# Two transformer-like blocks on one core: the value product in column halves, z gated from its bank, memories prepared at half rate, the second mixer's weight splits on VectorE

## What is computed

```python
# first block
x = x + hybrid_mixer(rms_norm(x), ...)
x = x + memory_cross_attention(rms_norm(x), rms_norm(mem), ...)
x = x + swiglu_ffn(rms_norm(x), ...)            # then rms_norm(x, norm_final_g)
# second block
x = x + 0.5 * swiglu(...)
x = x + concat([y_hgrn, y_conv]) @ w_out        # y_conv = zb * causal_conv3(zc * zu)
x = x + cross attention to a second memory
x = x + 0.5 * swiglu(...)                        # then rms_norm_2(x, final_norm)

# hybrid_mixer
z, xbc, dt_f, dt_b, q, k, v, gates = split_cols(h @ w_in, IN_SPLITS)
y = y_fwd + y_bwd + d_skip * xh                  # two state-space scans, forward and backward
v_ = (y * silu(z)) by 4 groups of 512 columns; v_ * rsqrt(mean(v_ * v_) + EPS) * g
out = softmax(q k^T, window of 128 and a sink) @ v        # 4 kv heads of 64, 4 q heads each
```

## Time and profile before

| | us |
|---|---|
| median of 3 runs | 2532.95 (2527.86 to 2536.98) |
| the profiled execution | 2534.28 |
| its span | 2532.5 |
| PE busy | 2462.1 (97%) |
| DVE, ACT, POOL busy | 1247.7 (49%), 1005.0 (40%), 394.6 (16%) |
| mean granted clock of PE | 0.989 |

### The profile page before, as it was taken

One profiled execution on the slowest core, in us unless ns is written; L12 is line 12 of the kernel. 1 busy time (PEld: TensorE's weight loads), 2 busy tenths in 40 slices (PEclk: granted clock), 3 DMA queues, 4 the chain that ended last, 5 costly groups with the idle time before them and its releaser, 6 DMA issues.

```text
span 2532.5 us, 29084 instructions
## 1 busy us (share of the span) xinstructions
PE 2462.1 (97%) x11416; PEld 1986.0 (78%) x11416; DVE 1247.7 (49%) x1843; ACT 1005.0 (40%) x1632; POOL 394.6 (16%) x283
## 2 busy tenths in 40 slices
PE   8999999898999999999999999999999999999998
PEld 7766668676888887888888788888887787888886
DVE  5577744457776454533333433423576644444422
ACT  6666653335455233423223322322634333332321
POOL 0000000054410010111102211101455300111101
PEclk9999999999999999999999999999999999999999
DMA  5221225223446331333332233322321222333231
GB/s 183 86 59 49 77 93 188 85 95 106 150 134 216 108 133 50 97 94 93 100 107 93 78 98 100 100 92 92 99 67 51 89 103 67 100 100 98 93 101 50
DMA packets 171337, 251.56 MB, mean 99 GB/s; under 512 B 11201, under 2 KB 88257, under 8 KB 171201
## 3 DMA queue, kind: packets, MB, share of 16 engines
q1 hardware_dynamic: 170768, 248.92, 31.0%
q10 hardware_dynamic: 432, 0.79, 0.1%
HBM read 231.83 MB, written 16.78 MB: 98 GB/s over the span
## 4 chain that ended last, share of the span: by engine, by line
PE 81%; DVE 8%; issue 5%; ACT 4%; DMA 1%; POOL 1%; POOLq 0%; SPq 0%; ACTq 0%; DVEq 0%
PE bank L1058 80%; DVE W L1817 1%; DVE T L1825 1%; DVE wlo L1817 1%; DMA scr_z<-T 1%; ACT whi L1384 1%; PE bank L1161 0%; ACT pr L1479 0%; DVE SC L2428 0%; DVE pr L1928 0%; POOL acc L2511 0%; ACT qs L1384 0%; DMA zb<-scr_z 0%; DVE T L1817 0%; ACT xp L1684 0%
## 5 line engine op out<-in xcount | busy, mean ns | idle before, releaser
L1058 PE MATMUL bank<-xh,whi 128*128 128x512 f32 x1784 | 716.2, 401 | 11.1 <-DVE wlo L1817 10.6
L1058 PE MATMUL bank<-xh,wlo 128*128 128x512 f32 x1784 | 698.5, 392 | 0.0
L1058 PE MATMUL bank<-xl,whi 128*128 128x512 f32 x1784 | 698.0, 391 | 0.0
L1817 DVE TENSOR_TENSOR wlo<-raw,whi 128x1024 fp32r<-128x1024 f32 (+2 forms) x382 | 472.4, 1241 | 332.3 <-ACT whi L1384 332.1
L1384 ACT ACTIVATE whi<-raw 128x1024 fp32r<-128x1024 f32 (+2 forms) x406 | 419.9, 1039 | 539.4 <-PE bank L1058 530.4
L1058 PEld LDWEIGHTS bank<-xh,whi 128*128 128x128 f32 x1784 | 337.1, 189 | 105.5 <-issue 27.2
L1058 PEld LDWEIGHTS bank<-xh,wlo 128*128 128x128 f32 x1784 | 336.7, 189 | 72.2
L1058 PEld LDWEIGHTS bank<-xl,whi 128*128 128x128 f32 x1784 | 337.5, 189 | 66.1 <-issue 1.0
L1817 DVE TENSOR_TENSOR T<-bank,R 128x512 f32<-128x512 f32 x90 | 61.8, 688 | 341.7 <-PE bank L1058 341.7
L1058 PE MATMUL bank<-hh,whi 128*128 128x512 f32 x528 | 205.4, 389 | 0.0
L1058 PE MATMUL bank<-hl,whi 128*128 128x512 f32 x528 | 205.4, 389 | 0.0
(11 more groups left out here) (340 smaller groups left out, 3614.2 us busy)
## 6 DMA issues: line engine op xcount, KB each, us to landing
raw<-in_w_in SPq DMA_DIRECT2D x92, 512.0 KB, 3.6
raw<-in_w_ffn_in SPq DMA_DIRECT2D x88, 256.0 KB, 3.2
raw<-in_ffn_gate SPq DMA_DIRECT2D x88, 256.0 KB, 2.8
raw<-in_ffn_up SPq DMA_DIRECT2D x88, 256.0 KB, 3.1
raw<-in_ffn_down SPq DMA_DIRECT2D x44, 512.0 KB, 3.5
raw<-in_w_ffn_out SPq DMA_DIRECT2D x22, 512.0 KB, 3.5
raw<-in_w_xattn_kv SPq DMA_DIRECT2D x16, 512.0 KB, 4.1
raw<-in_w_kv_mem SPq DMA_DIRECT2D x16, 512.0 KB, 4.0
```

The source lines that it names most:

```text
L1058: return e.matmul(out, l, r, start=start, stop=stop, skip_group_check=skip)
L1817: return e.tensor_tensor(out, a, b, op)
```

## The change

It has seven parts. (A) `pv` writes heads 0 and 2 to partitions 0 to 63 and heads 1 and 3 to 64 to 127, as two products of 256 columns each, and `o_out` is one copy. (B) `z_out` is a tanh straight from the bank with half of Rn as its scale (`Rh`, computed once on DVE), `z_silu` multiplies (tanh + 1) with the bank itself and frees it, and `z_gate` brings in the factor Rh in place of 0.5; one T is used for each tile. (C) Memory 1 is prepared at rate 4 with 8 and 3 empty points, in place of rate 8 with 16 and 7. (D) Memory 2 goes at rate 3 in place of 4; the memories' root is taken 5 points later, its spread one point after it and not two, and a group's `y_mean` and `y_scale` are not taken when its squares are ready, but just ahead of the next memory's root (the last group's when it is ready). (E) What is pending of these is written out between the scan's end and the mark "ssd", with `settle()`. (F) The second mixer's 24 wlo are on DVE; `c_out` multiplies by R², `u_out` multiplies the bank of hu with cu; the first tap is on ACT (`u_first`), the other two on DVE go straight to cu, and POOL's copy is gone; `h_states` stands at the first level of the next head, after its `select`. (G) The last norm's square 6 is added on DVE, not on POOL.

```diff
@@ z's ring, means @@
             soon(1, square)
             if c == 3:
-                soon(2, "y_mean", g)
-                soon(4, "y_scale", g)
+                soon(2, means.append, g)
+            if c == g == 3:
+                soon(2, mean)
+
+        def mean():
+            for g in means:
+                step("y_mean", g)
+                soon(2, "y_scale", g)
+            means.clear()
...
-            for _ in range(7):
+            for _ in range(3):
                 yield
             for k in range(8):
                 step("m_split", tag, k)
...
         def memory(tag):
-            late.append(norm(f"m{tag}", lag=2, among=ELSE))
+            first = norm(f"m{tag}", among=ELSE)
+            def root():
+                mean()
+                first()
+            late.append(lambda: soon(5, root))
...
-                start(prepare(2, 0), 4)
+                start(prepare(2, 0), 3)
...
-                start(prepare(1, 16), 8)
+                start(prepare(1, 8), 4)
...
             step("x_again")
+        mean()
+        settle()
         step("mark", "ssd")
...
             def conv():
-                tmp.new("uc", m)
-                step("u_conv", m)
+                step("u_first", m)
+                soon(1, "u_conv", m)
...
-                if li == 6 and h < 4:
+                h -= 1
+                if h >= 0 and h < 4 and li == 0:
                     side.new("hst", h)
                     step("h_states", h)
-                h -= 1
...
@@ pv, o_out @@
-                    ins = mm(b[0:64, :], v[:, k0 + j, kv * 64:kv * 64 + 64], pt[j][:], j == 0, j == k1 - k0 - 1)
+                    x = pt[j][:].rearrange("p (a b q) -> p a b q", a=2, b=2)
+                    for half in range(2):
+                        ins = mm(b[64 * half:64 * half + 64, 0:256], v[:, k0 + j, kv * 64:kv * 64 + 64], x[:, :, half, :],
+                                 j == 0, j == k1 - k0 - 1)
...
-                copy(q[0:64, 2 * kv:2 * kv + 2, chunk(n)], src[:, :, 0, :]).then_inc(*up("o_out", ("o half", i)))
-                copy(q[64:128, 2 * kv:2 * kv + 2, chunk(n)], src[:, :, 1, :]).then_inc(
+                copy(q[:, 2 * kv:2 * kv + 2, chunk(n)], b[:, 0:256].rearrange("p (a q) -> p a q", a=2)).then_inc(
...
@@ z_out, z_silu, z_gate @@
-                copy(t[:], b[:], Rn[:, m:m + 1]).then_inc(*up("z_act", ("z out", g, m), ("main", "free", u)))
-                w.wait_ge(*free(tmp, "tmp", n2))
-                w.wait_ge(*at("z out", g, m))
-                e.activation(t2[:], t[:], ACT.Tanh, scale=0.5).then_inc(*up("z_act", ("z tanh", g, m)))
+                e.activation(t[:], b[:], ACT.Tanh, scale=Rh[:, m:m + 1]).then_inc(*up("z_act", ("z tanh", g, m)))
...
-                stt(t[:], t2[:], 1.0, t[:], ALU.add, ALU.mult).then_inc(
-                    *up("z_silu", ("z silu", g, m), ("tmp", "free", n2)))
+                stt(t[:], t[:], 1.0, b[:], ALU.add, ALU.mult).then_inc(
+                    *up("z_silu", ("z silu", g, m), ("main", "free", u)))
...
-                stt(x, x, 0.5, z[:], ALU.mult, ALU.mult).then_inc(*up("y_scaled", ("z gated", g, c)))
+                stt(x, x, Rh[:, c:c + 1], z[:], ALU.mult, ALU.mult).then_inc(*up("y_scaled", ("z gated", g, c)))
...
@@ second mixer @@
-            weights(n, columns("w_in_2", i), 8, "mix2", "dve" if n == "hf" else "pool", nat=n == "hi")
+            weights(n, columns("w_in_2", i), 8, "mix2", nat=n == "hi")
...
-                tt(cu[:, m, :], b[:], R[:], ALU.mult).then_inc(*up("mixer2_in", ("c out", m), ("main", "free", u)))
+                tt(cu[:, m, :], b[:], R2[:], ALU.mult).then_inc(*up("mixer2_in", ("c out", m), ("main", "free", u)))
...
-                tt(t[:], b[:], R[:], ALU.mult).then_inc(*up("mixer2_in", ("u out", m), ("main", "free", u)))
-                w.wait_ge(*at("u out", m))
-                w.wait_ge(*at("c out", m))
-                tt(cu[:, m, :], cu[:, m, :], t[:], ALU.mult).then_inc(*up("mixer2_in", ("u in", m), ("tmp", "free", n)))
+                tt(t[:], b[:], cu[:, m, :], ALU.mult).then_inc(*up("mixer2_in", ("u out", m), ("main", "free", u)))
...
+            def u_first(m):
+                n, t = tmp("u", m)
+                w.wait_ge(*at("u out", m))
+                copy(cu[:, m, :], t[:], V("cw2", 3 * m + 2)).then_inc(*up("u_first", ("u conv", m, 0)))
...
@@ square on DVE @@
-                if k == 0 or tag in ("m1", "m2") or (k < 7 and tag != "mix") or tag == "fin":
+                if k == 0 or tag in ("m1", "m2") or (k != (6 if tag == "fin" else 7) and tag != "mix"):
                     return
```

More of the change, by code:

```diff
@@ L129, in build @@
         small = at_kb(116.5, [P, 64], name="small")
-        Rn, Rmn = small[:, 0:4], small[:, 4:6]
+        Rn, Rmn, Rh = small[:, 0:4], small[:, 4:6], small[:, 40:44]
         Rn1, Rn2, Rn3 = small[:, 8:12], small[:, 12:16], small[:, 16:20]
@@ L204, in build @@
         lbt = at_kb(205.25, [P, 8, 4], name="lbt")
+        R2 = at_kb(52, [P, S], name="R2")
         lb_, oml = lbt[:, 5, :], lbt[:, 6, :]
@@ L234, in build, with weights @@
         slots, G = [], {}
-        def weights(name, pieces, nk, X, lo="dve", nat=False, ntok=S, order=None):
+        def weights(name, pieces, nk, X, nat=False, ntok=S, order=None):
             n = sum(p[2] for p in pieces)
             ids = list(range(len(slots), len(slots) + nk // 2))
-            slots.extend((pieces, k, lo) for k in order or range(0, nk, 2))
+            slots.extend((pieces, k) for k in order or range(0, nk, 2))
             G[name] = dict(ids=ids, n=n, X=X, nat=nat, ntok=ntok, M=ntok // P if nat else n // P)
@@ L735, in evict @@
                 tmp.new("z", g, m)
-                tmp.new("zt", g, m)
                 step("z_out", g, m)
@@ L1394, in weight @@
             def weight(i):
-                pieces, k, lo = slots[i]
+                pieces, k = slots[i]
                 n = sum(x[2] for x in pieces)
@@ L1801, in scalar @@
                     "ffn_up": ffn_up, "bounds": bounds, "f_sig": f_sig, "f_log": f_log, "h_silu": h_silu,
-                    "i_out": i_out, "b_split": b_split, "level": level, "ends": ends, "ke_turn": ke_turn,
+                    "i_out": i_out, "u_first": u_first, "b_split": b_split, "level": level, "ends": ends, "ke_turn": ke_turn,
                     "h_read": h_read, "h_rms": lambda h: rms("h", h), "h_gate": h_gate, "fin_gain": fin_gain}
@@ L1829, in sinks @@
                 tt(gboth[:], V("fin", 0, 8), V("ffn1_2", 0, 8), ALU.mult).then_inc(*up("bounds", ("gboth",)))
+                w.wait_ge(*at("rn", "mix"))
+                ts(Rh, Rn, 0.5, None, ALU.mult).then_inc(*up("bounds", ("half rn",)))
             def weight(i):
-                pieces, k, lo = slots[i]
-                if lo != "dve":
-                    return
+                pieces, k = slots[i]
                 n = sum(x[2] for x in pieces)
@@ L2511, in tt @@
                 return e.tensor_tensor(out, a, b, op)
-            def weight(i):
-                pieces, k, lo = slots[i]
-                if lo != "pool":
-                    return
-                n = sum(x[2] for x in pieces)
-                w.wait_ge(*at("w hi", i))
-                tt(wlo[i % NH][:, :, 0:n], raw[i % NR][:, :, 0:n], whi[i % NH][:, :, 0:n].bitcast(F32), ALU.subtract).then_inc(
-                    *up("w_lo_pool", ("w lo", i)))
             def square(tag, k):
@@ L2524, in square @@
                 sums, width = SUMS[tag]
-                if k and (tag in ("m1", "m2", "mix") or k == 7):
+                if k and (tag in ("m1", "m2", "mix") or k == 7 or (tag == "fin" and k == 6)):
                     return
@@ L2600, in ffn_gate @@
                 tt(t[:], t[:], R[:], ALU.mult).then_inc(*up("ffn_gate", ("ffn gate", tag, j)))
-            def u_conv(m):
-                n, t = tmp("uc", m)
-                w.wait_ge(*at("u conv", m, 2))
-                e.tensor_copy(cu[:, m, :], t[:]).then_inc(*up("conv2_pool", ("u there", m), ("tmp", "free", n)))
             def b_out(m):
                 n, t = tmp("b", m)
-                w.wait_ge(*at("u there", m))
+                w.wait_ge(*at("u conv", m, 2))
                 w.wait_ge(*at("b in", m))
@@ L2641, in out @@
                 tt(xT[:, k, :], xT[:, k, :], R[:], ALU.mult).then_inc(*up("out_pool", ("out", k)))
-            does = {"w_lo": weight, "square": square, "weigh": weigh, "state": state_,
-                    "skip_x": skip_x, "across": across_, "ffn_gate": ffn_gate, "u_conv": u_conv, "b_out": b_out,
+            does = {"square": square, "weigh": weigh, "state": state_,
+                    "skip_x": skip_x, "across": across_, "ffn_gate": ffn_gate, "b_out": b_out,
                     "level_mul": level_mul, "ends": ends, "h_gate": h_gate, "out": out}
```

28 lines of the change are left out of this document (14 added, 14 removed).

## The result

The changed kernel takes 2489.62 us (median of 4 runs, 2488.48 to 2491.49) against 2530.72 before, measured beside it: a ratio of 0.9835, interval 0.9814 to 0.9856, or 41.1 us less. The forecast was 2500 with a range of 2488 to 2527. The profiled execution took 2489.67, its span is 2487.9, so profile to profile it is 44.6 us less; the profiled execution before lies 3.6 us above this median.

A forecast was written before the change was run, and what follows sets the result against it. PE, busy 97% of the span, was taken as the bound. The terms −16 −4 −6 −4 +5.5 −8 −0.3 sum to −32.8, from the median of 2532.95 to 2500.2, say 2500 us; range 2488 to 2527.

The forecast's parts named there:

- A: Value product, up to 388 us: column halves overlap on PE, −16 us, between 11.0 and 18.1.
- B: First z tiles: waits for T go, new waits for DVE's products come; −4 us, ends 0 and −5.
- C: Memory 1, 600 to 640 us: splits at half rate relieve stalls, the spread waits 1.2; −6 us, ends −3 and −10.
- D: Memory 2 and the groups' roots, 690 to 730 us: fewer stalls, spread waits 1.2; −4 us, ends 0 and −8.
- E: Before bs0: group 2's root leaves PE idle some 3.6 us and the clock probably falls; +5.5 us, ends +1 and +7.
- F: Second mixer: weight splits on DVE and later h_states cut PE's waits; −8 us, ends −14 and +3.
- G: The end: DVE takes over POOL's sum, for which PE waited 1.6 us; −0.3 us, ends 0 and −1.
- the likeliest case: Whole kernel: column halves overlap and the terms sum to −32.8; 2500 us, 2489 to 2511, chance 0.55.
- the first: Rival, value product: column halves do not overlap, so A is 0; 2516 us, chance 0.22.
- The second: Rival: halves overlap, but z, memories, bs0 and mixer give the rest back; −9 in all, 2524 us, chance 0.10.
- The third: Rival: halves do not overlap and the rest is at its low ends, +7; 2540 us, chance 0.06.
- The fourth: Rival, second mixer: DVE becomes the bound and PE waits for each split; F is +47, 2555 us, chance 0.07.

The follow-up runs named there:

- the three together: Changed kernel with group 2's root back in the scan, the memories' spreads one step later, and the last norm's square 6 on GpSimd: 2484.68 us.
- the pair of value product runs: Kernel before with only the value product changed: 2517.28 us; changed kernel with both column halves in partitions 0 to 63 and two copies: 2502.26 us.
- the root in the scan: Changed kernel with group 2's mean and scale written out within the scan, as soon as its squares are there: 2485.11 us.

## Why the prediction was right, and where its sizes were off

The kernel is faster, by the mechanism that was named first, and the likeliest case held: the column halves overlap. The result, 2489.6, lies in the range, and just inside the forecast case's own 2489 to 2511: it is at its lower edge. By the steps:

**A** was oversized by 2.7, and by 4.4 if the 1.7 of the clock at 289 is not counted for it. The step "half of 0.453 is 18.1, I take 16" was near the truth for PE's work, 15.4 (17.1 less that 1.7). What I left out is that DVE and ACT, with 100 us to spare on average, still are late for single instructions when PE arrives earlier. PE idles 4.1 us more: 1.2 for DVE's wlo, 1.1 for its st, 1.0 for ACT's pr and 0.9 for its `pt`. The rows are single waits like this one of the changed kernel for `pt`:

```profile
109.74 0.44 PE L1073 MATMUL bank<-pt,v 128*64 128x256 f32 x2 [1.22 <-ACT pt L1402]
```

Spare time of an engine, averaged over a stretch, excludes that it becomes the bound there, not that PE waits.

**B** was right in its mechanism to a tenth: 3.7 us of new wait was forecast from 488.36 − 484.63, and 3.61 measured. The estimate of 3.5 for the other three products was too high, one wait of 1.80 is all. In between PE ran at the lower clock (products 0.43 apart and not 0.23) and came later itself. So the 1.7 credited for a stretch at the lower clock did not come, 3.4 are lost to it before and after. It cost nothing here: in the kernels with h_states early and with the three together the clock does not fall in this stage, PE waits 7.6 us in place of 5.4, and the stage takes 124.7 us as against 124.8. What was missing is the relief for the memory's stage, 4.1, that the run of B alone showed. It hides in the changed kernel among C's gain, and is the larger part of it.

**C** and **D** came out at −6.5 and −6.3. C's size is luck: the pace of the splits, for which it stood, is worth at most 2.3, the sums still wait 2.56 of their 3.35 us for DVE's HF, and the rest came with B. The term of +1.2 for each spread was 2.31 and 0.78, 3.1 in place of 2.4: at memory 1 ACT had a weight slot of 1.05 in front of the table load. D was undersized by 2.3; it was costed at less than half of the 12.6 that the stretch loses, without a row that said so. Of its 6.3 only 1.6 are waits; 5.1 are time at the lower clock, which the trace before lost there and the changed kernel's did not. The trace with the old pace of memory 1, whose D is the same, has 4.7.

**E** was forecast at +5.5 and is +5.4, and the run without it gets 4.5 to 5 back. Its two terms hold as well: the gap grew from 0.98 to 4.57, by 3.6, and the clock fell in it.

**F** is the step that failed: "The ceiling is 13.6 idle and 4.7 of clock. I take −8." It gave 19.2, more than the ceiling and beyond the end of −14; 1.7 of it may be chance, since the same mixer took 183.5 us in two other traces. I had one wait, of 4.2, for which I could name the edit, and valued the rest by a half. The runs show three parts of 5 to 8 us each, none of which I had costed separately: h_states 7.9 and the splits 6.6 alone, the convolution 5.9 by its removal, or 4 to 5 each without the time at the lower clock. My fear, that 24 splits in DVE's queue would be late for PE, had no effect: PE's list of waits has no wlo in the mixer, and DVE is busy 117 of 165 us, 71%, where I had worked out 99 of 135, 73%. With no new wait to take their place, nearly all old ones went, and the three stretches at the lower clock behind them. One reading of the earlier trace rows was wrong: W is not "0.42 or 2.6 and little between". Of the 56, 35 take about 0.42 us, 13 about 1, 3 take 1.5 and 5 take 2.5 to 2.6; in the changed kernel 54 take 0.41 to 0.44. The mean of 801 and the saving worked out from it stand.

**G** was forecast at −0.3, and the waits are 2.08 in place of 2.41, which is −0.33. The measured +0.7 goes with the clock, which fell at 2474.1, ahead of the sums; of the seven other kernels that end in the same way six take 0.5 to 1.2 us less for the same tail, and the one with the old convolution 0.1 more.

The rivals: the first, halves one behind the other, fell with the pair of value product runs. The second, that the rest is given back, held for E alone. The third, both together, fell with the first. The fourth, DVE as the bound in the mixer, fell; its condition of 95% was never near. Two sums of the prediction are a little off and change nothing: the four places together are 57.6 us and not 60, and by its own terms the chance of less than 7.6 us either way is 0.11 and that of a slower kernel 0.10. That the result lies inside the range owes something to luck: A fell short by 2.7 and B to F gave 15 more, and a part of that is time at the lower clock.

## What to carry to other kernels

The value product, whose result has 64 rows, went to partitions 0 to 63 alone. With the moving side cut in two and the halves sent to different partitions, they ran side by side at 1.9 times the pace. Try it wherever a result has 64 rows.

Cost each edit of a stage by the wait that it takes away, and add them; in this mixer, where the engine that got the work stayed at 71%, the ceiling of the stage (its idle time and its lower clock) was a better estimate than half of it. In the z stage, where waits moved to DVE, it was not. Look for steps that a tidier order puts between two stages: the root before bs0 costs 5 us and no stage had needed it there. When two traces are compared stage by stage, put PE's idle time and the time at the lower clock beside the lengths: a gain that is only in the last column may not come again.

## What the runs showed of the hardware

Whether a stall brings the lower clock with it is in part chance. Up to 100 us all fourteen kernels give PE the same products, and each has a wait of about 1.87 us near 72. In eight of them the granted clock stays at 2.4 GHz behind it, in six it falls to 1.2 GHz for 3.4 us. The product that starts at 100.0 in the kernel before starts between 99.8 and 101.0 in the eight, and between 102.3 and 102.8 in the six. In the six the wait ends at 72.2 to 72.7, in the eight at 71.2 to 71.7 but for one at 72.4: a shift of 1 us that no edit asked for may decide it. The changed kernel and the one with the old pace (PE's columns as in the earlier trace rows):

```profile
60.00:90.00 30.00, 28.13 (x170) 24.08 (x170) 16.16 (x32) 21.08 (x34) 0.00 (x0) 1.00 0.46 134
```

```profile
60.00:90.00 30.00, 28.13 (x164) 24.57 (x162) 16.05 (x27) 20.70 (x32) 0.00 (x0) 0.94 0.40 127
```

Before bs0 two kernels have the same gap of 1.59 us, though not the same steps ahead of it. In the one with the root in the scan the clock stays at 2.4 GHz, in the one with the three together it falls:

```profile
752.00:770.00 18.00, 16.12 (x91) 13.03 (x90) 11.18 (x16) 12.94 (x24) 0.00 (x0) 1.00 0.36 117
```

```profile
752.00:770.00 18.00, 16.11 (x83) 13.01 (x82) 9.89 (x14) 12.25 (x22) 0.00 (x0) 0.91 0.37 117
```

The second loses 9% of 18 us, 1.6. So a difference of up to 2 us in one stage of two profiled executions says nothing by itself; the single waits do.
